# A decoder layer with 16,384 one-neuron experts: an eighth of the experts' first products moved into earlier stages, four accumulators kept in PSUM, one ring of banks for the rest

## What is computed

```
q      = h @ w_query                          # 8 heads x 2 halves x 128
i, j   = top 16 of each half's scores; the best 16 of their sums
gates  = softmax of the best 16 scores        # per token and head
act    = gelu(h . expert_u[i*128 + j])        # for each of 128 picks of a token
out    = sum over picks of gate * act * expert_v[i*128 + j]
x      = rmsnorm(x + g2 * out) * final_g
```

## Time and profile before

| | |
|---|---|
| median of three runs | 3413.57 us (3411.19 to 3413.98) |
| profiled execution | 3408.12 us, span 3406.4 us |
| TensorE busy | 3063.9 us (90%) |
| VectorE busy | 2764.3 us (81%) |
| ScalarE, GpSimd busy | 1075.3 us (32%), 1306.3 us (38%) |
| last scores of retrieval by TensorE | 1136 us |
| scatter's products begin | 1209 us |
| experts' first `share` begins | 1469 us |
| experts' last addition ends | 3364 us |

### The profile page before, as it was taken

The page is one execution under the profiler, slowest core; times in us unless marked ns, Lnnn a source line. Parts: engine busy times, 40 slices in busy tenths (PEclk is TensorE's granted clock), DMA queues, the critical chain, the costliest instruction groups (busy, mean ns, idle before and its releaser), DMA issues. The chain is left out here.

```text
span 3406.4 us, 54238 instructions
## 1 busy us (share of the span) xinstructions
PE 3063.9 (90%) x18245; PEld 2716.9 (80%) x18245; DVE 2764.3 (81%) x5532; ACT 1075.3 (32%) x1793; POOL 1306.3 (38%) x1716
## 2 busy tenths in 40 slices
PE   6999999998877255699999999999999999999993
PEld 4998888788766245589888999988899998889992
DVE  5464333564699999589999999999999999999998
ACT  4223666313333234322222222222222222222221
POOL 0001000010344300055555555555555555555555
PEclk9999999999988677799999999999999999999996
DMA  6445343233100046678888888888888888888886
GB/s 236 142 137 158 106 118 93 96 137 105 50 25 0 1 141 204 219 267 305 309 306 302 300 298 303 305 310 305 300 302 297 304 306 311 303 300 302 297 285 222
DMA packets 324671, 750.02 MB, mean 220 GB/s; under 512 B 19324, under 2 KB 166360, under 8 KB 324576
## 3 DMA queue, kind: packets, MB, share of 16 engines
q0 software_dynamic: 115712, 419.48, 34.3%
q1 hardware_dynamic: 207808, 325.16, 29.0%
q10 hardware_dynamic: 1056, 4.19, 0.3%
HBM read 681.61 MB, written 67.15 MB: 220 GB/s over the span
## 5 line engine op out<-in xcount | busy, mean ns | idle before, releaser
L1666 POOL DMA_INDIRECT ex_u_row<-in_expert_u,ex_row x384 | 452.9, 1179 | 161.1 <-issue 132.9
L1863 DVE SCALAR_TENSOR_TENSOR acc<-ex_v_row,ex_coef,acc 128x1024 f32<-128x1024 f32 x384 | 491.5, 1280 | 13.3 <-issue 4.8
L1670 POOL TENSOR_TENSOR ex_carry<-g_gate 128x1 f32<-128x1 f32 x765 | 251.0, 328 | 629.4 <-DVE ex_dot L1850 338.0
L1850 DVE CUSTOM_DVE_ANT_0 ex_u_row<-ex_u_row,ex_h_rows 128x1024 f32<-128x1024 f32 x384 | 467.5, 1217 | 2.2 <-DMA ex_u_row<-in_expert_u,ex_row 2.2
L1746 PE MATMUL psum<-ex_v_hi,ex_c_lo 128*128 128x512 f32 x1280 | 422.7, 411 | 7.5 <-DVE ex_v_lo L1845 4.9
L1893 DVE TENSOR_TENSOR acc<-psum,acc 128x512 f32<-128x512 f32 x640 | 426.3, 683 | 1.2
L1666 POOL DMA_INDIRECT ex_v_row<-in_expert_v,ex_row x384 | 387.4, 1009 | 55.7 <-issue 13.0
L1746 PE MATMUL psum<-ex_v_lo,ex_c_hi 128*128 128x512 f32 x1280 | 401.0, 394 | 0.0
L1746 PE MATMUL psum<-ex_v_hi,ex_c_hi 128*128 128x512 f32 x1280 | 396.7, 391 | 0.0
L1731 PE MATMUL psum<-h_hi,h_lo 128*128 128x320 f32 x2048 | 348.8, 313 | 3.2 <-DVE h_lo L1840 3.2
L1731 PE MATMUL psum<-h_lo,h_hi 128*128 128x320 f32 x2048 | 343.1, 310 | 0.0
(11 more groups left out here) (280 smaller groups left out, 5251.6 us busy)
## 6 DMA issues: line engine op xcount, KB each, us to landing
ex_un<-in_expert_u SPq DMA_DIRECT2D x64, 1024.0 KB
ex_vn<-in_expert_v SPq DMA_DIRECT2D x64, 1024.0 KB, 7.3
w_dram<-sc_w SPq DMA_DIRECT2D x10, 4096.0 KB, 13.5
ex_w<-w_dram SPq DMA_DIRECT2D x64, 640.0 KB
gm_wm<-in_w_mod SPq DMA_DIRECT2D x16, 1024.0 KB, 5.1
pj_raw<-in_w_in SPq DMA_DIRECT2D x11, 1024.0 KB, 7.6
qk_dram<-pj_staged_r POOLq DMA_DIRECT2D x32, 256.0 KB, 3.6
gt_raw<-in_w_in SPq DMA_DIRECT2D x16, 512.0 KB, 4.0
```

Of the source, the lines that this page charges most:

```text
L1666: nc.gpsimd.indirect_dma_start(to[:], None, all_rows, bass.IndirectOffsetOnAxis(row[s][:, col:col + 1], 0)).then_inc(done, 16)
L1670: nc.gpsimd.tensor_tensor(carry[:, n:n + 1], g_gate[:, 0, 0:1], g_gate[:, 0, 0:1], ALU.mult)
L1850: nc.vector.tensor_tensor_reduce(out=u_row[k % 3][:], in0=u_row[k % 3][:], in1=h_rows[:, k % 3, :], scale=1.0, scalar=0.0, op0=ALU.mult, o ...
L1863: nc.vector.scalar_tensor_tensor(out=to, in0=v_row[k % 3][:], scalar=coef[:, k:k + 1], in1=to, op0=ALU.mult, op1=ALU.add).then_inc(row_use ...
```

## The change

1. **Steps have a period of four, and every fourth has half the first layer.** In the steps 3, 7, ..., 63 only the first row of 128 experts is turned and hidden (`units(j)` is 2 and not 4). The second row's gelu output was made earlier and comes from DRAM (`load_pre`, one 320 KB transfer) into the tile `pre`, where `weigh` takes it. The loops of TensorE, ScalarE, VectorE and SP hold four steps in their body and not two; 15 iterations and four written-out steps at the end. GpSimd's loop is unchanged.
2. **The 16 rows of experts are computed ahead** (class `Ahead`): four jobs after retrieval's last scores, two in each of scatter's five iterations, two at scatter's end. A job is one load of 512 KB, eight transposes (`turn`), a high and a low split on ScalarE alone (`split`; between them TensorE subtracts the high part in the bank with two matmuls, `leave`), 48 matmuls of 320 columns (`hide`), two gelus and two stores.
3. **Order in retrieval's end.** The rows of the gathered tokens' activations are made here and not at the experts' start. ScalarE now does, after its last copies: six copies of those, the split of job 0, the exponentials of head 6, the split of job 1, `one_hot` of head 6, all gelus and splits of jobs 0 to 3, and last the exponentials of head 7.
4. **Scatter** has two buffers of each one-hot tile, and four banks.
5. **Four tiles of the sum stay in banks 4 to 7** from the first step to the last (cleared once, never evicted; the last stage reads them from PSUM). VectorE adds six tiles a step and not ten.
6. **One ring of banks 0 to 3** holds, in TensorE's order, hidden units, turned units and the six other shares. Each waits for the unit that had its bank four units earlier. In `share` the order is: a ring share, a turn, a kept share, four times; then two ring shares.

The core of the diff:

```diff
+    NKEPT = 4
+    NU = 2 * (DENSE // P) - NKEPT
+    PERIOD = 4
-    TURNS = (1, 3, 5, 7)
+    def units(j):
+        return 2 if j % PERIOD == PERIOD - 1 else 4
...
+            def step(i, j, held, hiding=True, turning=True):
+                s = j % 2
+                def take(kind, step_of, n):
+                    bank, unit = held.pop(0)
+                    freed(i, unit)
+                    held.append((bank, (kind, step_of, n)))
+                    return bank
+                if hiding:
+                    u_split(i, j + 1)
+                    for n in range(units(j + 1)):
+                        hide(n, take("hide", j + 1, n))
+                pe.wait_ge(c_lo, i * (4 * PERIOD) + (4 * j + 4 + PRIME))
+                pe.wait_ge(v_hi, i * PERIOD + (j + 1 + PRIME))
+                pe.wait_ge(v_lo, i * PERIOD + (j + 1 + PRIME))
                 for n in range(NU):
+                    share(s, NKEPT + n, core.bank[take("share", j, n)], False)
+                    if turning and n < units(j + 2):
+                        turn(i, j + 2, n, take("turn", j + 2, n))
+                    if n < NKEPT:
+                        share(s, n, core.bank[4 + n], True)
...
                 for n in range(NU):
-                    to = acc[:, n // 2, (n % 2) * HALF:(n % 2 + 1) * HALF]
+                    to = acc[:, (NKEPT + n) // 2, (n % 2) * HALF:(n % 2 + 1) * HALF]
                     dve.wait_ge(summed, c * NU + (n + 1 + PRIME))
...
+                    if turning and n < units(j + 2):
+                        split_u(i, j + 2, n, TURN_BANKS[j][n])
+                    if n % 2 == 0:
+                        row_dot(c, 3 + n // 2)
+                    else:
+                        row_add(c, n // 2)
```

In scatter:

```diff
                     last = pe.drain().then_inc(placed, 1)
+                    n, m = i * 2 + (JOB0 + g // 4), g // 4
+                    if g % 4 == 0:
+                        ahead.turn(pe, n, m, i + JOB0 // 2)
+                    elif g % 4 == 1:
+                        ahead.leave(pe, n, m)
+                    else:
+                        ahead.hide(pe, n, m, g % 4 - 2)
...
                 for s in range(2):
-                    sp.wait_ge(evicted, i * 2 * NG * 4 + ((s + 1) * NG * 4 + 8))
+                    ahead.load(sp, i * 2 + (JOB0 + 2 + s), s)
+                    for half in range(2):
+                        ahead.store(sp, i * 2 + (JOB0 + s), half)
+                    sp.wait_ge(evicted, i * 2 * NG * 4 + ((s + 1) * NG * 4 + 4))
```

and the unit of the work ahead:

```diff
+    def hide(self, pe, n, m, half):
+        pe.wait_ge(self.lo_out, n * 2 + 4)
+        pe.wait_ge(self.gelued, n * 2 + (half + 1))
+        at, to = slice(DENSE + m * P, DENSE + (m + 1) * P), slice(half * HD, (half + 1) * HD)
+        ops = [(a[:, k, at], b[:, k, to]) for a, b in ((self.h.lo, self.h.hi), (self.h.hi, self.h.lo), (self.h.hi, self.h.hi)) for k in range(KD)]
+        for i, (lhsT, rhs) in enumerate(ops):
+            last = self.nc.tensor.matmul(self.hide_bank[half][:, 0:HD], lhsT, rhs, start=i == 0, stop=i == len(ops) - 1)
+        last.then_inc(self.hidden, 1)
```

More of the change, by code:

```diff
@@ L54 @@
 BASE = 20992
+RETRIEVE = "retrieve"
 KEEP = 16512
@@ L1581, in _, with experts @@
                     sp.sem_inc(w_free[s], 1)
-def experts(nc, core, t, expert_u, expert_v, h, acc, g_row, g_gate):
+            for n in range(END0, END0 + 2):
+                for half in range(2):
+                    ahead.store(sp, n, half)
+def experts(nc, core, t, expert_u, expert_v, h, h_rows, acc, g_row, g_gate, ahead):
     PRIME = 24
@@ new lines, in share, with u_split @@
+            def share(s, n, out, kept):
+                tt, dh = n // 2, n % 2
+                ops = [(a[:, e, tt * P:(tt + 1) * P], b[:, e, dh * HALF:(dh + 1) * HALF]) for a, b in passes(ch[s], vh) for e in range(2)]
+                for m, (lhsT, rhs) in enumerate(ops):
+                    last = nc.tensor.matmul(out, lhsT, rhs, start=m == 0 and not kept, stop=m == len(ops) - 1, skip_group_check=kept)
+                if not kept:
+                    last.then_inc(summed, 1)
+            def u_split(i, j):
+                pe.wait_ge(u_hi, before(i, j, units(j) + PRIME))
+                pe.wait_ge(u_lo, before(i, j, units(j) + PRIME))
@@ L1757, in _ @@
             for q in range(4):
[L1758 to L1760 removed]
+                turn(0, 0, q, q)
+            u_split(0, 0)
+            for n in range(4):
+                hide(n, n)
             for q in range(4):
[L1762 to L1767 removed]
@@ L1768, in _ @@
-            share(NSTEP - 2, 0, False)
-            share(NSTEP - 1, 1, False)
+                freed(0, ("hide", 0, q))
+                turn(0, 1, q, q)
+            pe.wait_ge(cleared, 1)
+            LATEST = [(0, ("share", -1, 3)), (1, ("turn", 1, 3)), (2, ("share", -1, 4)), (3, ("share", -1, 5))]
+            with pe.Fori(0, NI) as i:
+                held = list(LATEST)
+                for j in range(PERIOD):
+                    step(i, j, held)
+                assert held == [(b, (kind, j + PERIOD, n)) for b, (kind, j, n) in LATEST]
@@ L1771, in _ @@
+            held = list(LATEST)
+            for j in range(PERIOD):
+                step(NI, j, held, j < PERIOD - 1, j < PERIOD - 2)
         @block.scalar
```

444 lines of the change are left out of this document (301 added, 143 removed).

## The result

The changed kernel is slower: 3466.59 us (median of 4 runs, 3455.47 to 3472.52) against 3412.38 (3410.99 to 3413.98). The ratio is 1.0155, interval 1.0128 to 1.0181. Forecast were 3342 us, 3306 to 3392, and "slower" had 8 of 100.

What follows compares the result with a forecast made beforehand. TensorE was taken to set the pace of the experts' loop, VectorE next. 3408.1 + 1 (retrieval) + 3 (scatter) - 1 (experts' start) - 74 (loop and end) = 3337 us profiled, so 3342 measured; range 3306 to 3392.

Steps and rivals of the forecast that it cites:

- The loop, where the wait moves: Experts' loop: a short step stalls TensorE 3.4 us, then nothing more holds it, so it saves 3.7 us, not 7.08.
- rival B: Experts' loop: VectorE is the bound in every step, row gathers come later; 48 us, 3390; chance 0.24 together with Rival A on TensorE.
- The short step's stall: Experts' loop, every fourth step: TensorE waits 3.4 us for VectorE's first addition; bounds 0 to 7.1 us.
- Retrieval's tail: Retrieval's end: the jobs made ahead there are nearly hidden, costing +1 us.
- The cover that was called thin: Retrieval's end: the last exponentials finish 1 to 3 us before VectorE needs them; slow clock would cost up to 15 us.
- Scatter: Scatter stage: TensorE takes in the jobs at 16.5 of 19 us at full clock; +3 us for the stage.
- The end: From the last hide's start to the last addition's end: 56 us where it was 61.1, so 5 us less.
- Rival A: Experts' loop: branching back costs 3.3 us in 15 iterations; on TensorE 50 us, 3392; chance 0.24 together with rival B.
- C: Experts' loop: no stall, the short steps keep all their saving, 3291 us; chance 0.09.
- D: Scatter: TensorE at half clock sets the pace, 112 us more, 3450; chance 0.05 whole, 0.09 in part.
- E: Experts' loop: the ring's bank waits serialise TensorE with VectorE, far above 3450 us; chance 0.01.
- VectorE's room: Experts' loop before the change: VectorE busy 28.69 of 30 us, so 1.3 us in 30 to spare.

Runs made afterwards that it cites:

- the best kernel: Changed kernel with a semaphore wait replacing GpSimd's drain after the index copy, and head 6's exponentials and one_hot ahead of two splits on ScalarE: 3357.04 us, ratio 0.9839.

## Why the prediction was wrong, point by point

- **The step that failed** stands in "The loop, where the wait moves": "Behind it TensorE is held for no more", since VectorE needs "2.3 to 2.7 for one (addition, u split, dot or row addition)". These terms have no wait for the rows that a dot or a row addition reads. The prediction put that wait at nothing, but for the upper bound of the stall and rival B. The working went through VectorE and TensorE, instruction by instruction, and never through GpSimd, which issues the gathers. The change moves the row work to the last six units of the step, right before the index copy, and in front of the copy's drain is then a gather whose issue ended 1.1 us earlier or less. VectorE waits 174 us for rows in the loop (2.2 before), and the whole costs 102 us (3466.6 against 3364.7). With it the loop is 51 us longer than before, without it 48 shorter.
- **Rival B** named late rows, with 48 us, but for another reason: DMA share going up to 0.90. It went down to 0.79. With the drain away it is 0.88 and VectorE waits 3.2 us for rows. So the mechanism of B was wrong, even if its symptom (long steps stall too) was right, and its price was less than half.
- **The short step's stall**, 3.4 us: 3.59 and 3.70 measured. Right.
- **What a stall costs beyond itself** was left out: 1.6 us of low clock behind each, 15 times, so 24 us. In the best kernel four steps take 116.2 us (1544.67 to 1660.87), where 114.5 were forecast and 119.4 were before. That is the 1.7.
- **Retrieval's tail**, +1: +7.3. The wait of `one_hot` behind the splits was worked out (1157.5; it came at 1159.85), and its end held against where VectorE needs the products (1173.68). What they do to VectorE in between was not asked. The cover that was called thin held by luck: the last gelu came 2 us late, and the last exponentials ended at 1196.78, later than the 1195.66 at which VectorE was forecast to ask, but VectorE was itself 7 us late. With `one_hot` in front and the drain kept, VectorE waits 0.33 us for them.
- **Scatter**: right in pace and clock. From its start to the second hide +3.7 for +2.
- **The end**: +2.2 in place of -5; in the best kernel it is -6.4 (3355.6 less 3258.76, its last hide, against 103.2), so this too went with the drain and retrieval's order.
- **Rival A**, a cost at the branch back: in the best kernel's loop from 1550 to 3350 us TensorE waits 15 times, 14 of them the stall of up to 3.70, and VectorE's waits for nothing that the profile shows are 0.5 us at the longest. So no cost of the branch back shows in this loop. **C** (no stall), **D** (slow clock in scatter) and **E** (ring serialises) didn't happen. E is shut out by a number: four hidden units with the same ring and the wait on the copy took 3408.
- **VectorE's room** of 1.3 us a step was an error of reading: busy time isn't occupied time. It didn't decide here, since the change takes 2.4 us a step from VectorE.

With the drain and retrieval's order mended, the forecast of 3342 would have been 15 us too low (3357.0), inside its own range. In that kernel's profile the loop is 48 us shorter than before (1456.56 to 3258.76, 1802.2 us for 1850.05) and not 69, and the clock behind the stalls (15 times 1.6, 24 us) is enough for the 21 that are missing. That term too was put at nothing without a reason. The range was too narrow for what it left out: an engine at 38% busy whose queue had never been followed.

## What to carry to other kernels

When a change moves work on one engine, follow every queue that waits for that work, with its drains, also on engines that are far from busy: slack there is what absorbs such waits, and busy share doesn't show it. On GpSimd, wait for the one instruction whose result you need; a drain behind gathers waits for the gathers. And an engine whose timeline shows hardly a wait for others has no slack, whatever its busy share says: VectorE here at 96% with a lighter TensorE, GpSimd at 63% in one step of four hidden units.

## What the runs showed of the hardware

- A drain of GpSimd behind indirect gathers lasted until their rows had moved: in the changed kernel's loop it took 4.9 to 9.9 us and ended 0.79 to 1.02 us after the last packet of the gathers, in each of 59 steps. Its least was 1.45 us, where the last gather's issue had ended 3.6 us before the copy. With rows of half the bytes the median was 4.6 us and not 6.4.
- Of the same gather, issuing took 0.98 to 1.1 us in most places, 1.8 to 2.0 in some. It took 2.9 only in the place right before the index copy, there in 27 of 59 steps of the changed kernel and in every step of the kernel before with the row work moved. Why, no run here shows.
- A cast of VectorE took 3.19 us for 0.29 and an addition 4.18 for 0.28 while GpSimd multiplied; searches (find, match) and MAX8 beside it were not slowed.
- After 3.70 us of idle time TensorE's granted clock was 0.58 for the next 4.0 us, where it had been 1.00 before (1.05 us for a pair of matmuls of 512 columns, 0.62 otherwise).
